# Six half slots of the split weights, 1028 words apart instead of 1024

## What is computed

```
h    = rms_norm(x, g) * (1 + scale) + shift          # 512 (or 256) x 1024
u    = square(relu(h @ w_mlp1))                      # w_mlp1: 1024 x 4096
x    = x + gate * (u @ w_mlp2)                       # w_mlp2: 4096 x 1024
q, k, v, ... = split_cols(h @ w_in)                  # and the other projections
```

## Time and profile before

| | us |
|---|---|
| three runs | 2668.87, 2670.94, 3187.37 |
| median | 2670.94 |
| the profiled execution, its own time | 2668.16 |
| its span, first to last instruction | 2666.4 |
| TensorE busy with matmuls | 2505.2 (94%) |
| TensorE loading weights | 2041.3 (77%) |
| VectorE busy | 1557.0 (58%) |
| ScalarE busy | 931.7 (35%) |

### The profile page before, as it was taken

The page is one execution under the profiler, slowest core; times in us unless marked ns, Lnnn a source line. Parts: engine busy times, 40 slices in busy tenths (PEclk is TensorE's granted clock), DMA queues, the critical chain, the costliest instruction groups (busy, mean ns, idle before and its releaser), DMA issues.

```text
span 2666.4 us, 45804 instructions
## 1 busy us (share of the span) xinstructions
PE 2505.2 (94%) x19622; PEld 2041.3 (77%) x19622; DVE 1557.0 (58%) x2412; ACT 931.7 (35%) x1599; POOL 115.6 (4%) x222
## 2 busy tenths in 40 slices
PE   6999977779999999999998999999999998999997
PEld 3777666667887788887777888888887766788886
DVE  3355577766666788854675556645445466544444
ACT  3344443323235223342553432222233254423322
POOL 0000001111100001000000000000000000000000
PEclk8999999989999999999999999999999999999999
DMA  6000000004653555411002123333321101222210
GB/s 278 32 32 1 33 3 4 4 4 166 222 210 129 178 193 190 174 44 59 5 32 80 64 95 127 127 127 127 127 95 44 64 32 65 94 101 115 100 64 32
DMA packets 32202, 244.88 MB, mean 92 GB/s; under 512 B 3616, under 2 KB 3776, under 8 KB 20992
## 3 DMA queue, kind: packets, MB, share of 16 engines
q1 hardware_dynamic: 11808, 164.83, 15.5%
q0 software_dynamic: 20192, 77.11, 9.1%
HBM read 239.83 MB, written 2.10 MB: 91 GB/s over the span
## 4 chain that ended last, share of the span: by engine, by line
PE 85%; DVE 9%; issue 3%; ACT 2%; DMA 1%; POOL 0%; DVEq 0%; ACTq 0%; POOLq 0%
PE ps L337 56%; PE ps L2190 2%; PE ps L2419 2%; PE ps L949 1%; PE ps L2447 1%; PE ps L2463 1%; PE ps L1370 1%; PE ps L367 1%; PE ps L905 1%; PE ps L2465 1%; PE ps L2464 1%; PE ps L369 1%; PE ps L368 1%; PE ps L950 1%; PE ps L951 1%
## 5 line engine op out<-in xcount | busy, mean ns | idle before, releaser
L337 PE MATMUL ps<-hh,ws 128*128 128x512 f32 x3216 | 751.7, 393 | 11.2 <-DVE hh L524 7.5
L337 PEld LDWEIGHTS ps<-hh,ws 128*128 128x128 f32 x3216 | 601.2, 188 | 143.9 <-issue 15.6
L318 ACT ACTIVATE ws<-raw 128x1024 fp32r<-128x1024 f32 x295 | 308.7, 1049 | 423.9 <-PE ps L337 390.8
L326 DVE TENSOR_TENSOR ws<-raw,ws 128x1024 fp32r<-128x1024 f32 x295 | 359.7, 1221 | 156.4 <-ACT ws L318 156.4
L337 PE MATMUL ps<-g,ws 128*128 128x512 f32 x1536 | 355.3, 390 | 0.0
L337 PEld LDWEIGHTS ps<-g,ws 128*128 128x128 f32 x1536 | 286.4, 188 | 58.0
L337 PE MATMUL ps<-gg,ws 128*128 128x512 f32 x960 | 221.5, 391 | 2.1 <-ACT ws L318 2.1
L1807 DVE SCALAR_TENSOR_TENSOR xT<-ps,mods,xT 128x512 f32<-128x512 f32 x120 | 90.0, 750 | 213.6 <-PE ps L337 206.3
L337 PEld LDWEIGHTS ps<-gg,ws 128*128 128x128 f32 x960 | 181.2, 189 | 40.6 <-ACT ws L318 2.4
L1970 DVE TENSOR_TENSOR sq<-sq 128x512 f32<-128x512 f32 (+1 forms) x128 | 80.0, 625 | 142.9 <-ACT sq L1947 142.9
L1947 ACT ACTIVATE sq<-ps 128x512 f32<-128x512 f32 (+1 forms) x128 | 69.3, 542 | 258.3 <-PE ps L337 244.3
(11 more groups left out here) (378 smaller groups left out, 3571.4 us busy)
## 6 DMA issues: line engine op xcount, KB each, us to landing
raw<-in_w_m SPq DMA_DIRECT2D x32, 2048.0 KB, 7.8
raw<-in_w_ada POOLq DMA_DIRECT2D x80, 512.0 KB, 3.9
raw<-in_w_mlp SPq DMA_DIRECT2D x16, 2048.0 KB, 7.9
ar<-in_w_ada POOLq DMA_DIRECT2D x48, 512.0 KB, 3.9
raw<-in_w_in SPq DMA_DIRECT2D x8, 2048.0 KB, 7.7
raw<-in_w_mg SPq DMA_DIRECT2D x8, 1536.0 KB, 7.2
raw<-in_w_out SPq DMA_DIRECT2D x6, 2048.0 KB, 8.0
raw<-in_w SPq DMA_DIRECT2D x5, 2048.0 KB, 7.9
```

The costliest lines, as they stand in the source:

```text
L318: e.activation(w_of(n)[0], pieces[n][2], ACT.Copy).then_inc(*hi(n))
L326: e.tensor_tensor(l, pieces[n][2], h.bitcast(F32), ALU.subtract).then_inc(*lo(n))
L337: m = e.matmul(o, a, b, start=n == 0, stop=n == 3 * kt - 1)
```

## The change

The row of each half slot becomes 1028 words long, of which the first 1024 are used as before. A spare tensor of 8 words stands behind `ws`.

```diff
-        ws = sb("ws", [P, WSN, 2, 1024], F32R)
+        ws = sb("ws", [P, WSN, 2, 1028], F32R)
+        sb("gapw", [P, 8])
```

## The result

The changed kernel takes 2695.61 us (median of 4 runs, 2691.88 to 2702.63), the kernel before on the same chip 2669.9 us. The ratio is **1.0112**, 95% interval 1.0096 to 1.0128: 1.1% slower, and 3.6 us above the upper end of the forecast range. The profiled execution is the slowest of the four: 2702.63 us, 34.5 us more than the one before.

The account below looks back on a forecast made before the run. TensorE's dense matmul stream was taken to bound the kernel. Each of four points added 0 to the profiled 2668 us; with the runs' median 2.8 us higher, the forecast was 2670 us, range 2652 to 2692.

Parts of the forecast that it names:

- What bounds the kernel: TensorE's dense matmul stream: 2505.2 of 2666.4 us busy; a change counts through what one matmul costs.
- Point 4: Everything behind `ws` moves 128 bytes, same place modulo 64: 0, at most 0.4 us, from DMAs.
- The prediction's own sign of being wrong: Wrong if distances between matmul starts (226 to 228 ns wide, 120 narrow) or split times have two levels.
- Point 1: TensorE weight loads starting off a multiple of 64 bytes, 5040 of 9072: 0, bounds 16 us either way.
- Point 2: ScalarE and VectorE splits at shifted addresses in `ws`: stay at 1047 and 1224 ns, 0, bound 2.4 us.
- point 3: `ws` as moving operand in the value projections: 0, judged from a shifted moving operand in the trace.
- Rival A: Off-64 loads fetch each line twice; narrow matmuls lose 134 us, wide ones are covered: 2805 us; chance 0.07.
- Rival B: Fixed part vanishes where TensorE's weight load is off 64: 66 us less, 2605 us; chance 0.05.
- Rival C: If `ws` starts off 64, another pair of halves is aligned: 2670 us, part of the 0.88 for no change.
- the fixed part of 13 ns: Time of each dense-stream matmul beyond its columns, 12 to 15 ns, about equal for wide and narrow, taken as 13.

Follow-up runs that it names:

- the 64 bytes: The kernel before with 64 spare bytes behind `ws`: 2676.22 us, ratio 1.0030.
- the moved narrow operands: The kernel before with only the second block's narrow moving operands (`hc2`, `gc2`) moved 192 bytes further on: 2660.21 us against 2666.07, ratio 0.9977.

## Why the prediction was wrong, point by point

*What bounds the kernel.* Right in what counts: the loss is in the distance between matmuls of the dense stream. 16.4 + 8.8 + 4.3 - 0.5 - 1.2 = 27.8 us are in the five groups above and 1.2 us more in `yy`, and the late part of the trace grew by 28.6 us. The remainder of the 34.5 us between the profiled executions lies mostly in the small products, whose time varies from trace to trace; the median over runs moved by 25.7 us. One reading was wrong, without effect on the sum: PEclk has an 8 in the ninth slice as well as in the first, the very stretch of those products.

*Point 4, everything behind `ws` 128 bytes further on.* **This step failed.** It took modulo 64 for the whole of what an address can matter, found the moving operands "at the same place", and priced only DMAs (0 to 0.4 us). The runs show in its place that the 128 bytes alone cost 26 us (1.0099 of 2668), which is the whole loss. They move the moving operands against the weights by half a period of 256 bytes, and a wide matmul then takes 232 to 233 ns instead of 226.7. The same 128 bytes ahead of `ws`, where nothing moves against the weights, cost nothing (1.0007), and the price of the DMAs did not show. The prediction's own sign of being wrong came true: the distances have more than one level (226 to 241 ns).

*Point 1, loads off 64.* The value 0 was wrong, and the mechanism behind its bound is not what the runs show: loads at +32 are off 64 as well, and with the moving operand at +32 too they cost nothing. The rows it was taken from could not show it. The shifted matmul of the earlier trace rows is of plain float32, some 430 ns from pass to pass, and no dense stream of float32r. The halves' starts by themselves, beside moving operands that stay at 0 modulo 256, are worth 17 us by the medians and 19 by the ratio (1.0072); beside the 128 bytes they add nothing that can be measured. The bound of 16 us was thus near in size by chance, since it did not foresee that wide matmuls with aligned loads lose as well.

*Point 2, the splits, and point 3.* The splits: right, 1048 and 1224 ns as before. Point 3 (the moving `ws` of the value projections) took 0 from the same, which could not show it either; the group at line 2190 went from 44.8 to 45.8 us of busy time, a small amount that no run tells from chance.

*Rival A* (each line fetched twice, narrow ones hit, wide ones covered) came out the other way round: wide ones got longer and narrow ones shorter. *Rival B* had the right place, TensorE's two reads and their relative start, and the wrong sign: agreement is the best place for wide ones. The argument against it, that all matmuls of the kernel have one and the same relative start so that no row shows another, was in truth a reason for more doubt on both sides. The Trainium skill's sentence quoted there (TensorE: Matmul & The Clock Gate), that the two operands have ports of their own, does not mean here that the two reads leave each other alone: with all else still, a shift of the one changes the pace by 3%. Nor does its isolated gap of N / 2.4 + 2.5 ns appear at any start tried: the least wide distance is 226.7 ns, not 215.8, the least narrow one 113.3, not 109.2.

*Rival C* is excluded: its time was that of the forecast, and the offsets between halves act (0.72% alone).

*The numbers.* Within 2% is what came, but the range was built as if the unseen price had an upper bound from one mechanism. A dense stream of 7000 matmuls turns 1 ns into 7 us; the fixed part of 13 ns was left unexplained in the prediction, and a price of 6 to 7 ns on every wide matmul, half of it, was all it took.

What stays open: which mechanism makes the distance depend on the relative start modulo 256 bytes, why one pair of starts has several stable patterns, why a start at 16 bytes costs even where both operands have it, and why narrow ones take 113.3 ns at +64 but not at +320. That the relative start makes the loss is shown; by what mechanism is not.

## What to carry to other kernels

Where one engine streams two operands from on-chip memory back to back, the starts of the two relative to each other are a parameter of the kernel, down to a few bytes (shown here for TensorE and float32r alone) and with a period well above 64; a spare tensor anywhere between them moves it. Look at the distances between starts in a dense stretch: a list that repeats with the buffers points to their starts. A constant distance is not yet the good one, since 226.7 and 233.3 ns both ran constant. A short kernel with only the stream maps the offsets in one run. Its numbers gave the time to within 2 us for the 64 bytes and for the moved narrow operands, and 4 us too much where the halves were 1028 words apart with 256 bytes behind (2690 forecast, 2685.87 measured).

## What the runs showed of the hardware

- Float32r matmuls with 128 x 128 weights at the full clock: 226.7 ns for 512 columns and 120.0 for 256 where weights and moving operand start at the same place modulo 256 bytes (not where both are at +16: 233.3 and 118.3). Elsewhere up to 234.4 ns for the wide ones (weights at +96 bytes) and down to 113.3 for the narrow ones (at +64). One word (4 bytes) is enough to leave the first: 232.3 ns.
- Several constant distances are multiples of 16 columns' time over the columns: 113.3 ns is 256 + 16 columns at 2.4 GHz, 120.0 is 256 + 32, 226.7 is 512 + 32, 233.3 is 512 + 48, 173.3 is 384 + 32.
- The same starts can give two paces: 228.9 and 233.3 ns in one execution of the kernel with 64 bytes, each for hundreds of matmuls on end. With high and low at 0 and 16 bytes it was 226.9 and 232.1 ns in one execution of the kernel with 1028 words and 256 bytes.
- Fewer columns of weights don't shorten a wide matmul: 229.9 ns with 64 columns of weights at agreeing starts, against 226.7 with 128.
